# Feed-forward sums in a decoder step: three of four accumulating transfers of each pair's first half of rows are cut in two

## The chip, the cores and the metric

One core of one Trainium2 chip. The metric is the device time of one execution in microseconds (us). Engines as the profile names them: PE (TensorE, matmul), PEld (its weight loads), DVE (VectorE), ACT (ScalarE), POOL (GpSimd) and SP (SyncE). Transfers run on 16 DMA engines.

## The reference, cut to what matters

One layer of a recurrent decoder, for 1024 new tokens of a prompt and 8 single tokens (1032 tokens together), model width 1024, feed-forward width 2816, everything in float32:

```
x = x + 0.5 * swiglu(rmsnorm(x, n1), f1g, f1u, f1d)     # first feed-forward
h = rmsnorm(x);  proj = h @ w_in                        # mixer: two recurrent branches, gates
x = x + m @ w_out
x = x + 0.5 * swiglu(rmsnorm(x, n3), f2g, f2u, f2d)     # second feed-forward
y = rmsnorm(x, final_norm)

def swiglu(x, w_gate, w_up, w_down):
    return (silu(x @ w_gate) * (x @ w_up)) @ w_down
```

The change touches the two feed-forwards alone, and in them the way in which the products with w_down reach x.

## The kernel before, in words

**Layout and tiles.** Activations lie transposed: x is 8 tiles of 128 rows (of the model width) by 1032 tokens. The tokens are taken in two halves of 516 (HW), each as two banks of 258. The feed-forward width is 22 tiles of 128, taken in 11 pairs (PAIRS). Every float32 product is three matmuls with split operands (`three`, lines 149 to 156: high by high, high by low, low by high).

**A pair.** For pair i TensorE makes the gate products, then the down products of the pair before, then the up products. Each set is made with seven block products in place of eight (a 2 x 2 block scheme), whose results VectorE and ScalarE put together: ScalarE copies a bank into a tile (`snap`, line 921; `down_part`, line 929), VectorE adds another bank to it (`mix`, line 1080; `down_part`, line 1088). Pair 0 and the last pair's down products go another way, so 9 groups (i = 2 to 10) of each feed-forward have such a down stage, 18 in all. The groups 2 to 9 are a loop on TensorE, ScalarE and VectorE; GpSimd's list is written out.

**The down stage.** Its result has 8 tiles of rows. They are made in two halves, c = 0 (tiles 0 to 3, "the first half of rows") and c = 1. In each half the seven products j = 0 to 6 run, each for q = 0 and then q = 1 (which two of the four tiles), and give four parts, kind 0 to 3 (a tile of the two, a half of the tokens). A part is a tile of 128 x 2 x 516 numbers, the middle index being q. The parts of c = 0 and c = 1 share their buffers `s.part[kind]`, except that kind 2 of c = 1 lies in `snap_t[:, 1:3]`, which the up products' copies use right after (line 921, n = 1 and 2).

**Adding to x.** x itself is overlaid by other tiles while the pairs run. Ahead of them GpSimd copies x into x_sum in HBM (line 1258, eight transfers of 516 KB), and each finished part is added there by an accumulating transfer that GpSimd issues (line 1269), in the order c = 0 kinds 0, 1, 2, 3, then c = 1 kinds 0, 1, 2, 3. Each waits until both q of its part are done: kinds 0 to 2 for VectorE's sum (semaphore `mixed`), kind 3 for ScalarE's copy (`snap`). At the end SP reads x_sum back into x (lines 1316 to 1319).

**Who waits for a transfer.** Each kind has a semaphore `x_added[kind]`, 16 for each transfer landed. ScalarE's `down_part` waits on it ahead of line 929, so that a part's buffer isn't written over while it is being sent: a copy for c = 1 waits for the transfer of c = 0 of its kind (not kind 2, whose c = 1 buffer is another), a copy for c = 0 for the pair before. ScalarE's `snap` of the up products (line 921, n = 1, 2) waits for kind 2 of c = 1. TensorE then waits for these copies (`chain_wait`, `product7`): the second up product (j = 1) for the copies of kind 3, c = 1, and the fifth (j = 4) for the copy n = 1 of line 921. VectorE (line 1112, pair 1), ScalarE (line 835) and SP wait on the same semaphores once in a feed-forward.

**The other traffic.** SP loads the weights in slabs of 512 KB into two buffers (line 1280), each when the buffer is free.

Of the kernel before, what the change touches and what calls it, by code (L numbers as in the profile page):

```python
# [19 lines left out]
ALU = mybir.AluOpType  # L20
# [15 lines left out]
PAIRS = FT // 2  # L36
# [19 lines left out]
HW = T // 2  # L56
# [4 lines left out]
FIRST_PRODUCTS = 8  # L61
LAST_DOWN = 3
DOWN_PAIRS = ((3, 2), (1, 0))
ADDED = 32 * (PAIRS - 1)
PARTS = ((0, 0), (1, 1), (1, 0), (0, 1))
HIDDEN_FIRST = ((0, 0), (0, 1), (1, 0), (1, 1))
HIDDEN = ((0, 0), (1, 1), (1, 0), (0, 1))
# [203 lines left out]
def half(h):  # L271

    return slice(h * HW, (h + 1) * HW)
# [7 lines left out]
def halves(ap):  # L281

    return ap.rearrange("p (g q) -> p g q", g=2)


def both(k, pair):

    return k.pair[pair][:, :, 0:QW]


def is_one(i):

    return isinstance(i, int) and i == 1


def units(i, n):

    return FIRST_UNITS + n if is_one(i) else i * 21 + (n + FIRST_UNITS + 14 - 42)


def prods(i, n):

    return FIRST_PRODUCTS + n if is_one(i) else i * 42 + (n + FIRST_PRODUCTS + 14 - 84)


def summed(i, n):

    return n if is_one(i) else i * 12 + (n + 8 - 24)


def snaps(i, n):

    return n if is_one(i) else i * 22 + (n + 6 - 44)


def mixes(i, n):

    return n if is_one(i) else i * 18 + (n + 6 - 36)
# [14 lines left out]
def prod_number(i, up, j):  # L333
    return (0, 7 if is_one(i) else 35)[up] + j + 1
# [6 lines left out]
def mix_number(i, up, n):  # L341
    return (0, 3 if is_one(i) else 15)[up] + n + 1


def down_prod(c, j, q):
    return 7 + 14 * c + 2 * j + q + 1


def down_snap(c, n, q):

    return 3 + 8 * c + 2 * n + q + 1


def down_mix(c, n, q):

    return 3 + 6 * c + 2 * n + q + 1
# [467 lines left out]
def hidden_part(i, n):  # L824
    return (HIDDEN_FIRST if i == 0 else HIDDEN)[n]


def hidden_high(act, k, s, i, n):

    f, h = hidden_part(i, n)  # L830
    act.wait_ge(s.hidden, i * 4 + (n + 1))
    if i and n == 0:
        act.wait_ge(k.x_added[1], s.added_base + ADDED)
        act.wait_ge(k.x_added[2], s.added_base + ADDED - 16)
    act.activation(s.hid_hi[:, f, half(h)], s.gt[:, f, half(h)], ACT.Copy).then_inc(s.hidden_hi, 1)


# [7 lines left out]
def hid_f(s, j):  # L845

    return s.hb_f[:, 2 * HID_IN.get(j, j) + 1, :]
# [34 lines left out]
def ffn_scalar(act, k, s):  # L882
# [31 lines left out]
    def snap(i, up, n):  # L914
        act.wait_ge(s.prod, prods(i, prod_number(i, up, (0, 2, 3)[n])))
        if up:
            act.wait_ge(s.mixed, mixes(i, (1, 3, 2)[n]))
            if n and not is_one(i):
                act.wait_ge(k.x_added[2], i * 32 + s.added_base)
        pair = ((0, 0, 1), (2, 2, 1))[up][n]  # L920
        act.activation(halves(s.snap_t[:, n, :]), both(k, pair), ACT.Copy).then_inc(s.snap, 1)

    def down_part(i, c, n, q):

        kind = (0, 2, 1, 3)[n]
        act.wait_ge(s.prod, prods(i, down_prod(c, (0, 2, 3, 6)[n], q)))
        act.wait_ge(k.x_added[kind], i * 32 + (s.added_base - 32 + (16 * c if kind != 2 else 0)))
        pair = DOWN_PAIRS[c ^ (n == 2)][q]
        act.activation(halves(part(s, c, kind)[:, q, :]), both(k, pair), ACT.Copy).then_inc(s.snap, 1)  # L929

# [10 lines left out]
    def group_one():  # L941
        i = 1
        for j in range(2, 6):
            unit_high(act, k, s, i, 0, j)
        snap(i, 0, 0)
        unit_high(act, k, s, i, 0, 6)
        unit_high(act, k, s, i, 2, 0)
        snap(i, 0, 1)
        silu(i, 0)
        unit_high(act, k, s, i, 2, 1)  # L950
        snap(i, 0, 2)
        unit_high(act, k, s, i, 2, 2)
        unit_high(act, k, s, i, 2, 3)
        silu(i, 1)
        unit_high(act, k, s, i, 2, 4)
        silu(i, 2)
        silu(i, 3)
        unit_high(act, k, s, i, 2, 5)
        unit_high(act, k, s, i, 2, 6)
        behind_up(i, False)  # L960
# [76 lines left out]
def ffn_vector(dve, k, s):  # L1037
# [52 lines left out]
    def hidden(i, n, last):  # L1090

        f, h = HIDDEN[n]
        gt = s.gt[:, f, half(h)]
        dve.wait_ge(s.silu, i * 4 + (n + 1))
        if n < 3:
            dve.wait_ge(s.mixed, mixes(i, mix_number(i, 1, n)))
            other = s.snap_t[:, (0, 2, 1)[n], :]
        else:
            dve.wait_ge(s.prod, prods(i, prod_number(i, 1, 6)))
            other = both(k, 2)  # L1100
        if last:
            if n == 3:
                gt = halves(gt)
            dve.tensor_tensor(gt, gt, other, ALU.mult).then_inc(s.hidden, 1)
            return
        to = hid_f(s, (B11, B22, B21, B12)[n])
        if n == 3:
            gt, to = halves(gt), halves(to)
        if is_one(i) and n == 0:
            for kind in range(4):  # L1110
                dve.wait_ge(k.x_added[kind], s.added_base + 32)
        dve.scalar_tensor_tensor(to, gt, 0.5, other, ALU.mult, ALU.mult).then_inc(s.hidden, 1)

    def add(first, t, m):
# [123 lines left out]
def part(s, c, kind):  # L1238

    return s.snap_t[:, 1:3, :] if c == 1 and kind == 2 else s.part[kind][:, :, :]  # L1240


def x_block(s, c, kind):

    e, h = PARTS[kind]
    return s.x[:, 4 * c + e:4 * c + e + 3:2, half(h)]


def x_sum_block(s, c, kind):
    return s.x_sum[4 * c + kind].rearrange("p (q t) -> p q t", q=2)  # L1250


def ffn_gpsimd(pool, k, s):

    pool.wait_ge(s.down_used, NT * KT)
    for c in range(2):
        for kind in range(4):
            pool.dma_start(x_sum_block(s, c, kind), x_block(s, c, kind)).then_inc(k.x_added[kind], 16)
    for kind in range(4):
        pool.wait_ge(k.x_added[kind], s.added_base + 32)  # L1260

    def group(i):
        for c in range(2):
            for kind in range(4):
                if kind < 3:
                    pool.wait_ge(s.mixed, mixes(i, down_mix(c, kind, 1)))
                else:
                    pool.wait_ge(s.snap, snaps(i, down_snap(c, 3, 1)))
                pool.dma_start(s.x_sum[4 * c + kind], part(s, c, kind).rearrange("p q t -> p (q t)"), accum_op=ALU.add)\
                    .then_inc(k.x_added[kind], 16)  # L1270

    for i in range(2, PAIRS):
        group(i)


def ffn_sync(sp, k, s, behind_first=None, behind_second=None):

    def load(number, buf):
        src = k.w_slabs[bass.ds(number, 1)].rearrange("a p c -> p (a c)")
        sp.dma_start(k.raw[buf][:, :], src).then_inc(k.slab_loaded[buf], 16)  # L1280

    s.raw_free(sp, 0)
    load(s.first, 0)
    if behind_first:
        behind_first()
    s.raw_free(sp, 1)
    load(s.first + 1, 1)
    if behind_second:
        behind_second()
    for c in range(2, FIRST_SLABS):  # L1290
        sp.wait_ge(s.unit_lo, 2 * c - 2)
        load(s.first + c, c % 2)

    for c, done in enumerate((FIRST_UNITS - 1, FIRST_UNITS)):
        sp.wait_ge(s.unit_lo, done)
        load(s.first + FIRST_SLABS + c, c)
    for c, done in enumerate((2, 6)):
        sp.wait_ge(s.unit_lo, units(1, done))
        if c == 0:
            sp.wait_ge(s.sums, summed(1, 4))  # L1300
        load(s.first + FIRST_SLABS + 2 + c, c)

    def row(i, n, c):
        sp.wait_ge(s.unit_lo, units(i, 7 * (n - 1) + (2, 6)[c]))
        if c == 0:
            sp.wait_ge(s.sums, summed(i, 4 * n))
        load(i * 6 + (s.first - 2 + 2 * n + c), c)

    for i in range(2, PAIRS):
        for n in range(3):  # L1310
            for c in range(2):
                row(i, n, c)
    for c in range(2):
        row(PAIRS, 0, c)
    sp.wait_ge(s.prod, prods(PAIRS - 1, 35))
    for kind in s.back_order:
        sp.wait_ge(k.x_added[kind], s.added_base + ADDED)
        for c in range(2):
            sp.dma_start(x_block(s, c, kind), x_sum_block(s, c, kind)).then_inc(k.x_back[PARTS[kind][1]], 16)

# [1703 lines left out]
def build(nc, x_t, w_slabs, lru_w, vec, state_hgrn, state_lru, state_conv, consts,  # L3024
          y_out, hgrn_p, hgrn_s, lru_out, conv_p, conv_s):
    k = Names(w_slabs=w_slabs, state_hgrn=state_hgrn, hgrn_p=hgrn_p, hgrn_s=hgrn_s, lru_w_in=lru_w)
# [213 lines left out]
    with ExitStack() as ctx:  # L3240
# [3 lines left out]
        def sem(name):  # L3244
            return ctx.enter_context(nc.semaphore(name))
# [17 lines left out]
        hidden_hi, hidden_lo = sem("hidden_hi"), sem("hidden_lo")  # L3263
# [1 line left out]
        k.x_back = [sem("x_back"), k.consts_loaded]  # L3265

        def ffn(n):
            return dict(hidden_hi=hidden_hi, hidden_lo=hidden_lo, hid_base=8 * n, added_base=ADDED * n,
                        back_base=(64 * n, 32 + 64 * n), x_sum=x_sums[n])
        par = stage("par", "arg exp", steps=0)  # L3270
        n1 = stage("n1", "squared squared_vector added rstd_step " + HEAD, gain=G1, x=k.x1, x_loaded=x_loaded,
# [225 lines left out]
```

## Time and profile before

| | |
|---|---|
| Time, median of 3 runs | 2433.44 us (2432.48 to 2433.78) |
| The profiled execution | 2431.43 us, span 2429.6 us |
| PE busy | 2415.5 us (99%) |
| DVE, ACT, POOL busy | 1740.3 (72%), 1298.9 (53%), 171.9 us (7%) |
| Granted TensorE clock | 0.999 of full speed |
| q0, GpSimd's transfers | 23040 packets, 84.55 MB, 18.3% of 16 engines |
| q1, SP's transfers | 114128 packets, 192.39 MB, 24.2% |
| x_sum transfers of parts | 126 (f_part) and 18 (f_snap), 516 KB each |

The span is the profiled part of the execution; the execution's own time has some 2 us around it. Matmuls overlap (each is shown with some 0.28 us, while one starts every 0.12 us), so a stop of TensorE is seen in the starts. A row of a timeline gives start, duration, engine, line, operation, tiles, and in brackets the idle time before it and what ended it. GpSimd's rows are issues: the time that it spends on one, not the transfer.

### The profile page before, as it was taken

To read this page: it belongs to the slowest core of one execution; us is meant where nothing else is said; L and a number is where in the kernel's file an instruction comes from. 1 tells how busy PE (TensorE), PEld (TensorE's weight loads), DVE (VectorE), ACT (ScalarE), POOL (GpSimd) and SP (SyncE) were. 2 spreads that over 40 slices of the span, in tenths; PEclk is the share of its full clock that TensorE was granted. 3 is DMA by queue.
4 is the path that set the end of the run, shared out by engine and by line. 5 is a ranking of instruction groups with operands and counts; after the bars stand their busy time and mean duration, and the time that the engine had idled before them with its cause. 6 is when DMAs were issued, how large, how long until landed. Compare 5 with 4: busy or idle time off the path is not lost.

```text
span 2429.6 us, 51528 instructions
## 1 busy us (share of the span) xinstructions
PE 2415.5 (99%) x19220; PEld 2401.3 (99%) x19220; DVE 1740.3 (72%) x2921; ACT 1298.9 (53%) x2206; POOL 171.9 (7%) x204
## 2 busy tenths in 40 slices
PE   9999999999999999999999999999999999999998
PEld 8999999999999999999999999999999999999997
DVE  8767777777689888787777775442676777777777
ACT  5355555555568676676666664211434555555554
POOL 0011111111120000000000000000200111111110
PEclk9999999999999999999999999999999999999999
DMA  3355555555541343333222235332033555555556
GB/s 144 106 123 121 121 121 121 122 121 122 142 175 54 97 113 79 87 97 107 105 87 87 73 140 180 138 126 87 18 106 90 121 122 123 121 123 123 122 123 194
DMA packets 137270, 278.34 MB, mean 115 GB/s; under 512 B 67024, under 2 KB 71632, under 8 KB 136656
## 3 DMA queue, kind: packets, MB, share of 16 engines
q1 hardware_dynamic: 114128, 192.39, 24.2%
q0 software_dynamic: 23040, 84.55, 18.3%
q8 instruction: 69, 1.13, 0.2%
q14 instruction: 33, 0.27, 0.0%
HBM read 154.80 MB, written 114.77 MB: 111 GB/s over the span
## 4 chain that ended last, share of the span: by engine, by line
PE 97%; DVE 1%; ACT 1%; DMA 1%; issue 0%; SPq 0%; DVEq 0%; ACTq 0%
PE banks L154 31%; PE banks L155 31%; PE banks L156 31%; PE banks L1817 1%; PE banks L1848 1%; PE banks L1838 1%; PE banks L1852 1%; PE banks L1846 1%; DMA x_sum<-f_part 0%; DVE y L247 0%; DVE f_blk_f L502 0%; DVE f_blk_lo L526 0%; DMA raw<-w_slabs 0%; PE banks L238 0%; PE banks L240 0%; ACT f_blk_hi L518 0%
## 5 line engine op out<-in xcount | busy, mean ns | idle before, releaser
L154 PE MATMUL banks<-f_blk_hi,f_u_hi 128*128 128x258 f32 x2496 | 706.6, 283 | 1.1 <-ACT f_part L929 0.7
L155 PE MATMUL banks<-f_blk_lo,f_u_hi 128*128 128x258 f32 x2496 | 705.7, 283 | 0.0
L156 PE MATMUL banks<-f_blk_hi,f_u_lo 128*128 128x258 f32 x2496 | 704.8, 282 | 0.0
L154 PE MATMUL banks<-mix_blk_hi,mix_u_hi 128*128 128x258 f32 x1808 | 515.1, 285 | 0.7 <-DVE mix_blk_lo L526 0.4
L155 PE MATMUL banks<-mix_blk_lo,mix_u_hi 128*128 128x258 f32 x1808 | 511.0, 283 | 0.0
L156 PE MATMUL banks<-mix_blk_hi,mix_u_lo 128*128 128x258 f32 x1808 | 510.2, 282 | 0.0
L154 PEld LDWEIGHTS banks<-f_blk_hi,f_u_hi 128*128 128x128 f32 x2496 | 471.4, 189 | 2.5 <-ACT f_part L929 0.9
L156 PEld LDWEIGHTS banks<-f_blk_hi,f_u_lo 128*128 128x128 f32 x2496 | 471.2, 189 | 0.0
L155 PEld LDWEIGHTS banks<-f_blk_lo,f_u_hi 128*128 128x128 f32 x2496 | 470.9, 189 | 0.2
L154 PEld LDWEIGHTS banks<-mix_blk_hi,mix_u_hi 128*128 128x128 f32 x1808 | 342.0, 189 | 1.4 <-issue 1.1
L155 PEld LDWEIGHTS banks<-mix_blk_lo,mix_u_hi 128*128 128x128 f32 x1808 | 341.6, 189 | 0.1
L156 PEld LDWEIGHTS banks<-mix_blk_hi,mix_u_lo 128*128 128x128 f32 x1808 | 341.4, 189 | 0.0
L154 PE MATMUL banks<-f_hb,f_u_hi 128*128 128x258 f32 x1008 | 285.3, 283 | 0.0
L155 PE MATMUL banks<-f_hb,f_u_hi 128*128 128x258 f32 x1008 | 284.9, 283 | 0.0
L156 PE MATMUL banks<-f_hb,f_u_lo 128*128 128x258 f32 x1008 | 284.5, 282 | 0.0
L1088 DVE TENSOR_TENSOR f_part<-banks,f_part 128x516 f32<-128x516 f32 x180 | 125.0, 695 | 152.8 <-PE banks L156 148.6
L929 ACT ACTIVATE f_part<-banks 128x516 f32<-128x516 f32 x252 | 151.1, 602 | 103.9 <-PE banks L156 79.4
L155 PEld LDWEIGHTS banks<-f_hb,f_u_hi 128*128 128x128 f32 x1008 | 191.1, 190 | 0.0
L156 PEld LDWEIGHTS banks<-f_hb,f_u_lo 128*128 128x128 f32 x1008 | 190.5, 189 | 0.0
L154 PEld LDWEIGHTS banks<-f_hb,f_u_hi 128*128 128x128 f32 x1008 | 190.3, 189 | 0.0
L800 DVE TENSOR_TENSOR f_u_lo<-f_sum,f_u_hi 128x512 fp32r<-128x512 f32 x232 | 156.0, 687 | 42.8 <-ACT f_u_hi L794 42.5
L794 ACT ACTIVATE f_u_hi<-f_sum 128x512 fp32r<-128x512 f32 x232 | 140.8, 626 | 84.7 <-PE banks L156 47.8
(306 smaller groups left out, 4378.0 us busy)
## 6 DMA issues: line engine op xcount, KB each, us to landing
raw<-w_slabs SPq DMA_DIRECT2D x220, 512.0 KB, 3.5
x_sum<-f_part POOLq DMA_DIRECT2D x126, 516.0 KB, 7.8
x_sum<-f_snap POOLq DMA_DIRECT2D x18, 516.0 KB, 10.1
x_sum<-x POOLq DMA_DIRECT2D x16, 516.0 KB, 5.7
x<-x_sum SPq DMA_DIRECT2D x16, 516.0 KB, 8.2
sg_kept<-sgt SPq DMA_DIRECT2D x8, 1032.0 KB, 5.6
sgs<-sg_kept SPq DMA_DIRECT2D x16, 516.0 KB, 4.5
x_kept<-x SPq DMA_DIRECT2D x1, 4128.0 KB, 12.1
```

The lines of the kernel that those rows point to most:

```text
L154: pe.matmul(out, wh, xh, start=start, stop=False, skip_group_check=chained)
L155: pe.matmul(out, wh, xl, start=False, stop=False, skip_group_check=chained)
L156: return pe.matmul(out, wl, xh, start=False, stop=stop, skip_group_check=chained)
L794: act.activation(s.u_hi[j][:, :], unit_source(k, s, n, j), ACT.Copy).then_inc(s.unit_hi, 1)
L800: dve.tensor_tensor(s.u_lo[j][:, :], unit_source(k, s, n, j), s.u_hi[j][:, :].bitcast(F32), ALU.subtract)\
L929: act.activation(halves(part(s, c, kind)[:, q, :]), both(k, pair), ACT.Copy).then_inc(s.snap, 1)
L1088: dve.tensor_tensor(to, both(k, pair), to, ALU.add).then_inc(s.mixed, 1)
L1817: last = pe.matmul(k.bank[5][:, 0:P], s.ke[:, tok], s.qe[:, tok], start=True, stop=True)
L1838: pe.matmul(k.bank[6][:, at], s.kt[:, n, :], s.v[:, n, :], start=True, stop=True).then_inc(s.u_ready, 1)
L1846: pe.matmul(o[:, 0:P], s.s[n % 2][:, :], s.qe[:, n * P:(n + 1) * P], start=True, stop=False, skip_group_check=True)
L1848: last = pe.matmul(o[:, 0:P], s.v[:, n, :], s.sc[n % 2][:, :], start=n == 0, stop=True, skip_group_check=True)
L1852: last = pe.matmul(o[:, P + b:P + b + 1], s.ss[:, b, :], s.qe[:, SEQ + b:SEQ + b + 1], start=True, stop=True, skip_group_check=True)
```

## The change

Kinds 0, 1 and 3 of c = 0 are sent in two transfers of 258 KB each, one for each q, each as soon as its q is ready; kind 2 of c = 0 and all of c = 1 stay whole. A pair then has 11 accumulating transfers in place of 8. The semaphores count 48 a pair for kinds 0, 1 and 3 and 32 for kind 2 (`ADDS`), and all waits on them are put on the new counts: a copy for c = 1 waits for both halves of c = 0.

```diff
-ADDED = 32 * (PAIRS - 1)
+ADDS = (48, 48, 32, 48)
+ADDED = tuple(32 + adds * (PAIRS - 2) for adds in ADDS)
...
     if i and n == 0:
-        act.wait_ge(k.x_added[1], s.added_base + ADDED)
-        act.wait_ge(k.x_added[2], s.added_base + ADDED - 16)
+        act.wait_ge(k.x_added[1], s.added_base[1] + ADDED[1])
+        act.wait_ge(k.x_added[2], s.added_base[2] + ADDED[2] - 16)
...
             if n and not is_one(i):
-                act.wait_ge(k.x_added[2], i * 32 + s.added_base)
+                act.wait_ge(k.x_added[2], i * ADDS[2] + s.added_base[2])
...
-        act.wait_ge(k.x_added[kind], i * 32 + (s.added_base - 32 + (16 * c if kind != 2 else 0)))
+        added = s.added_base[kind] + 32 - 2 * ADDS[kind] + (32 * c if kind != 2 else 0)
+        act.wait_ge(k.x_added[kind], i * ADDS[kind] + added)
...
+    def done(i, c, kind, q):
+        if kind < 3:
+            pool.wait_ge(s.mixed, mixes(i, down_mix(c, kind, q)))
+        else:
+            pool.wait_ge(s.snap, snaps(i, down_snap(c, 3, q)))
+
     def group(i):
         for c in range(2):
             for kind in range(4):
-                if kind < 3:
-                    pool.wait_ge(s.mixed, mixes(i, down_mix(c, kind, 1)))
+                to = s.x_sum[4 * c + kind]
+                if c == 0 and kind != 2:
+                    for q in range(2):
+                        done(i, c, kind, q)
+                        pool.dma_start(to[:, q * HW:(q + 1) * HW], part(s, c, kind)[:, q, :], accum_op=ALU.add)\
+                            .then_inc(k.x_added[kind], 16)
                 else:
-                    pool.wait_ge(s.snap, snaps(i, down_snap(c, 3, 1)))
-                pool.dma_start(s.x_sum[4 * c + kind], part(s, c, kind).rearrange("p q t -> p (q t)"), accum_op=ALU.add)\
-                    .then_inc(k.x_added[kind], 16)
+                    done(i, c, kind, 1)
+                    pool.dma_start(to, part(s, c, kind).rearrange("p q t -> p (q t)"), accum_op=ALU.add)\
+                        .then_inc(k.x_added[kind], 16)
```

The remaining lines of the diff put the same new counts into the waits of VectorE (line 1112), SP (line 1316) and the start of GpSimd's list.

## Rows read from the trace of the kernel before

**Rows 1.** The page: busy time by engine; the chain that ended last, by engine
```profile
PE 2415.5 (99%) x19220; PEld 2401.3 (99%) x19220; DVE 1740.3 (72%) x2921; ACT 1298.9 (53%) x2206; POOL 171.9 (7%) x204
...
PE 97%; DVE 1%; ACT 1%; DMA 1%; issue 0%; SPq 0%; DVEq 0%; ACTq 0%
```

**Rows 2.** Waits of TensorE, whole span: us in total, times, longest
```profile
PE banks L154 <- ACT f_part L929: 0.7, 1, 0.7
```

**Rows 3.** Timeline of PE around 1889 us
```profile
1888.94 0.28 PE L155 MATMUL banks<-f_blk_lo,f_u_hi 128*128 128x258 f32 x1
1889.06 0.28 PE L156 MATMUL banks<-f_blk_hi,f_u_lo 128*128 128x258 f32 x1
1890.04 0.39 PE L154 MATMUL banks<-f_blk_hi,f_u_hi 128*128 128x258 f32 x1 [0.70 <-ACT f_part L929]
```

**Rows 4.** Timeline of ACT, the same pair
```profile
1888.89 1.09 ACT L929 ACTIVATE f_part<-banks 128x516 f32<-128x516 f32 x2 [3.18 <-DMA x_sum<-f_part]
```

**Rows 5.** Timeline of POOL: the copies of x; one pair; the late pair
```profile
89.07 2.29 POOL L1258 DMA_DIRECT2D x_sum<-x  x3 [87.14 <-DVE x L1120]
93.89 0.70 POOL L1258 DMA_DIRECT2D x_sum<-x  x1 [2.53 <-issue]
...
217.70 0.84 POOL L1269 DMA_DIRECT2D x_sum<-f_part  x1 [2.98 <-DVE f_part L1088]
...
220.50 0.85 POOL L1269 DMA_DIRECT2D x_sum<-f_part  x1 [0.48 <-ACT f_part L929]
223.47 0.85 POOL L1269 DMA_DIRECT2D x_sum<-f_part  x1 [2.12 <-DVE f_part L1088]
...
229.25 0.88 POOL L1269 DMA_DIRECT2D x_sum<-f_snap  x1 [0.60 <-DVE f_snap L1088]
232.57 0.85 POOL L1269 DMA_DIRECT2D x_sum<-f_part  x1 [2.45 <-issue]
...
1877.44 0.84 POOL L1269 DMA_DIRECT2D x_sum<-f_part  x1 [0.46 <-ACT f_part L929]
```

**Rows 6.** Us to landing, issues at 89.07, 217.70, 220.50, 223.47, 229.25, 1877.44
```profile
x_sum<-x POOLq DMA_DIRECT2D x1, 516.0 KB, 4.5
...
x_sum<-f_part POOLq DMA_DIRECT2D x1, 516.0 KB, 5.4
...
x_sum<-f_part POOLq DMA_DIRECT2D x1, 516.0 KB, 7.7
...
x_sum<-f_part POOLq DMA_DIRECT2D x1, 516.0 KB, 8.7
...
x_sum<-f_snap POOLq DMA_DIRECT2D x1, 516.0 KB, 9.5
...
x_sum<-f_part POOLq DMA_DIRECT2D x1, 516.0 KB, 11.4
```

**Rows 7.** Timeline of DVE, the pair around 217 us
```profile
215.93 2.85 DVE L1088 TENSOR_TENSOR f_part<-banks,f_part 128x516 f32<-128x516 f32 x4 [0.62 <-PE banks L156]
```

**Rows 8.** Queues' packets, MB, share: windows 221 to 223, 91 to 93, 668 to 670
```profile
q0 software_dynamic: 115, 0.41, 107.8%
...
q0 software_dynamic: 174, 0.65, 96.6%
...
q1 hardware_dynamic: 412, 0.81, 104.9%
```

**Rows 9.** All waits of line 921; its copies and PE's next matmuls, two pairs
```profile
ACT f_snap L921 <- DMA x_sum<-f_snap: 64.5, 18, 4.1
...
238.87 0.60 ACT L921 ACTIVATE f_snap<-banks 128x516 f32<-128x516 f32 x1 [2.92 <-DMA x_sum<-f_snap]
...
240.88 0.28 PE L154 MATMUL banks<-f_blk_hi,f_u_hi 128*128 128x258 f32 x1
...
2079.45 0.60 ACT L921 ACTIVATE f_snap<-banks 128x516 f32<-128x516 f32 x1 [4.08 <-DMA x_sum<-f_snap]
...
2080.29 0.29 PE L154 MATMUL banks<-f_blk_hi,f_u_hi 128*128 128x258 f32 x1
```

More of the change, by code:

```diff
@@ L1110, in hidden @@
             for kind in range(4):
-                dve.wait_ge(k.x_added[kind], s.added_base + 32)
+                dve.wait_ge(k.x_added[kind], s.added_base[kind] + 32)
         dve.scalar_tensor_tensor(to, gt, 0.5, other, ALU.mult, ALU.mult).then_inc(s.hidden, 1)
@@ L1259, in ffn_gpsimd @@
     for kind in range(4):
-        pool.wait_ge(k.x_added[kind], s.added_base + 32)
+        pool.wait_ge(k.x_added[kind], s.added_base[kind] + 32)
+    def done(i, c, kind, q):
[3 more added lines that the diff above has]
+            pool.wait_ge(s.snap, snaps(i, down_snap(c, 3, q)))
     def group(i):
@@ L1316, in ffn_sync @@
     for kind in s.back_order:
-        sp.wait_ge(k.x_added[kind], s.added_base + ADDED)
+        sp.wait_ge(k.x_added[kind], s.added_base[kind] + ADDED[kind])
         for c in range(2):
@@ L3267, in ffn @@
         def ffn(n):
-            return dict(hidden_hi=hidden_hi, hidden_lo=hidden_lo, hid_base=8 * n, added_base=ADDED * n,
+            return dict(hidden_hi=hidden_hi, hidden_lo=hidden_lo, hid_base=8 * n, added_base=tuple(added * n for added in ADDED),
                         back_base=(64 * n, 32 + 64 * n), x_sum=x_sums[n])
```

## The prediction

> **What bounds the kernel now.** I read the page's totals and chain first, then the waits of TensorE, then the timelines around the transfers that change, then their landings.
>
> The reader is to see that TensorE is never done: busy 2415.5 of 2429.6 us and 97% of the chain of waits, with VectorE, ScalarE and DMA at 1% each [rows 1]. So the change can only pay by removing idle time of TensorE, and cost by making some. In the list of TensorE's waits just one entry has to do with the changed transfers: one wait of 0.7 us, for line 929, the copy of a finished part out of a bank [rows 2]. It lies in the second feed-forward, in the first of its pairs that has a down product. Up to there one matmul starts every 0.12 us (1888.94, 1889.06); the next starts at 1890.04 instead of 1889.18, so 0.86 us are lost [rows 3]. ScalarE explains it: at 1888.89 it begins the two copies of part 3 for the second half of rows, after 3.18 us of waiting for an x_sum transfer, and 1.09 us later (1889.98) they are done [rows 4]. That transfer is part 3 of the first half of rows, issued at 1877.44 [rows 5] and landed 11.4 us later, at 1888.84 [rows 6].
>
> I write K0 to K3 for the four transfers of the first half of rows and K0' to K3' for those of the second. The change splits K0, K1 and K3.
>
> **The change, part by part.** I take the first feed-forward's pair around 217 us as the pattern; 17 of the 18 pairs show no loss on TensorE. K0 goes 2.98 + 0.85 us ahead of K1 [rows 5] and is nearly out when K1's data come: its split moves nothing behind it.
>
> *The earlier first halves.* VectorE's four part instructions from 215.93 take 2.85 us, 0.71 each [rows 7]; the second ends at 217.36 and K1 is issued at 217.70 [rows 5]. The first half of K1 is ready 0.71 us sooner and can go at 216.99. The issue keeps GpSimd 0.84 us, so the second half goes at about 217.84, 0.14 later than K1 now. K1 lands 5.4 us after its issue, at 223.1 [rows 5, 6]. K3 (220.50 + 7.7) lands at 228.2, so K2 and K3 follow K1 in 5.1 us, 2.55 each [rows 5, 6]: from K1 on the transfers stand in line and the DMA engines set the pace.
>
> *Cost of a half on the engines.* The trace has no accumulating row piece of 2,064 bytes. From three windows of 2 us: accumulating pieces of 4,128 bytes take 1.078 x 2 us x 16 engines / 0.41 MB = 84 engine-us per MB, 0.35 us each; plain pieces of 4,128 bytes 0.966 x 2 x 16 / 0.65 = 48 per MB; plain pieces of 2,064 bytes (x read back) 1.049 x 2 x 16 / 0.81 = 41 per MB [rows 8]. Plain pieces are thus not dearer by the byte when they are halved. Below, a halved accumulating piece costs 0.35 x 41/48 / 2 = 0.15 us (each split K gains 8 x 2 x 0.025 = 0.4 us); above, as much as a whole one, 0.35 (each split K costs 8 x 0.35 = 2.8 us more). I take half, 0.175, being nearest to the plain rows: a split costs nothing in line.
>
> *When K1 and K3 then land.* A half alone should land 5.4 - 1.3 = 4.1 us after its issue: the first at 221.1, the second 1.35 us behind at 222.4 against 223.1, 0.65 us earlier. K2 and K3 follow, 0.65 us earlier too.
>
> *What GpSimd's queue adds.* GpSimd seems to have room for three transfers: of the eight plain copies the first three go back to back from 89.07 and the fourth at 93.89, 0.32 us after the first landed (89.07 + 4.5); K3' is ready early but goes at 232.57, 0.40 us after K0' landed (223.47 + 8.7) [rows 5, 6]. If a half takes a place like a whole, the first half of K3 waits for that of K1 (221.1 + 0.3 = 221.4), the second for the second of K1 (222.7), and K0' for K2 (225.75 - 0.65 + 0.3 = 225.4, now 223.47). A transfer alone spends 5.4 - 2.7 = 2.7 us outside its service, so their data are ready at the latest at 224.1, 225.4 and 228.1, while the line before them is worked on until about 225.1, 226.4 and 227.5. Only K0' can find an empty line, for 0.6 us at most, which gives back what was won. Behind the held issues on GpSimd stand only its own later transfers. So K2' comes between 0.65 us earlier and no later than now.
>
> *Who waits for that.* K2' is the transfer with the least room: every pair ScalarE's copy on line 921 waits for it, 64.5 us in 18 times, up to 4.1 [rows 9]. After the 2.92 us wait the copy ends at 238.87 + 0.60 = 239.47 and the matmul that needs its bank starts at 240.88, 1.41 us spare; after the 4.08 us wait it is 2080.05 against 2080.29, 0.24 us spare [rows 9]. Spare time is thus 4.32 less the wait, 0.74 us in the mean (64.5 / 18 = 3.58). An earlier K2' gives nothing: TensorE doesn't stall there. It is what hides the 54 added issues (18 pairs x 3); once it is used up, each us later costs up to 18 us.
>
> *The rest.* GpSimd gets 54 x 0.85 = 46 us more issue time, three in the pair; it has 2 to 3 us idle between issues [rows 5], and nothing else sits on it in these stretches. ScalarE, VectorE and SP wait as often as before, on other numbers; ScalarE's copies for the second half now need both halves landed, which is when they needed the whole. I put these at nothing.
>
> *The sum.* The late pair: its K1 to K3 go 0.65 us earlier, K3 at 1888.2, copies done at 1889.3, matmul at 1889.4, so 0.2 of the 0.86 us stay: 0.66 us won, once. Against the profiled execution: 2431.43 (span 2429.6 and 1.8 around it) - 0.66 = 2430.8. The median of the runs, 2433.44, lies 2.0 above the profiled one; on that scale 2432.8.
>
> The Trainium skill has a rule against splitting: "DMA: Bandwidth & Descriptors", section on the anatomy of one SWDGE DMA, gives a transfer issued by GpSimd a fixed 2.0 us plus its bytes at 436 GB/s, 3.2 us for 516 KB. The trace agrees for a transfer alone (5.4 us, more even) and not for one in line, 2.55 us behind the one before [rows 5, 6].
>
> **Rivals.**
> 1. *The loss stays.* The one late K3 is late because the line in that pair is slow as a whole (11.4 us against 7.7 [rows 6]), and held issues eat the head start. For: it happens in 1 of 18 pairs, which the size of a transfer doesn't explain. Against: K1 is ahead of it in any case. Time 2433.4, or 1 us either way.
> 2. *Slower: three places are too few.* K0' held for K2, or K3's halves for K1's, leaves the engines empty more than I computed, in all pairs. It decides from an empty 0.65 + 0.74 = 1.4 us a pair on, where K2' comes 0.74 us late and spare time is gone in the mean; single pairs pay from 0.9. At 2 us it costs about 18 x (2 - 1.4) = 11 us: 2444; at 1.4 some 3 us: 2436. For: the holds in rows 5. Against: 2.7 us of work stands in line when a place comes free.
> 3. *Slower: a halved piece costs like a whole one.* Two splits stand ahead of K2' in the line (K1, K3): 2 x 2.8 - 0.65 = 4.9 us later, 18 x (4.9 - 0.74) = 75 us: 2508. Against: plain pieces go by the byte [rows 8].
> 4. *A fixed time for each added transfer in line.* If two more starts were paid ahead of K2' as a transfer alone pays (2.7 us outside its service each), 5.4 - 0.65 - 0.74 = 4.0 us a pair, 72 us: 2505. Against: K2 and K3 pay no such time now. By the 2.0 us that the Trainium skill gives in "DMA: Bandwidth & Descriptors" it would be 18 x (2 x 2.0 - 0.65 - 0.74) = 47 us: 2480.
>
> **How the numbers follow.** Forecast 0.62; rival 1 0.20; rival 2 0.11; rivals 3 and 4 together 0.06; something faster that I don't see 0.01, as no more than 0.86 us of TensorE's idle time hangs on these transfers. A measurement tells 0.2%, 4.9 us, from no change. The forecast, rival 1 and half of rival 2 are inside it: 0.88; slower 0.11; faster 0.01. The range goes from 2430.6 (all 0.86 us won, and two us for the spread between medians) to 2438.0 (rival 2 up to its middle).
>
> **What would show it.** GpSimd should show 198 accumulating issues, 108 halves (258 KB) and 90 wholes, for the 144 now, of some 0.85 us each. In the pair around 217 us K1's second half should land near 222.4, K3's near 227.5, and K2' not after 238.75 (229.25 + 9.5 [rows 5, 6]); the wait of line 921 on x_sum should be at or under 64.5 us in sum. The price of a 2,064-byte accumulating piece, read as above from a window of the line: 84 engine-us per MB or less if I am right, near 170 if rival 3 is. K0' should be seen to go about 0.3 us after K2 lands if places are counted by transfer, at 223.47 if by bytes. TensorE's one wait on line 929 should shrink to some 0.2 us or go, with no new entry on line 921 or 929. The prediction is wrong if TensorE waits on line 921 or 929 in several pairs, or if the time leaves the range; if the time fits and the 0.7 us wait is still there, its mechanism is wrong and rival 1 right.

## The result, and the profile after

Changed, the kernel takes 2482.98 us (median of 5 runs, 2479.79 to 2487.96) against 2432.48 (5 runs, 2431.72 to 2433.78): a ratio of 1.0207, 95% interval 1.0196 to 1.0219. Some 50 us are lost. 2432.8 was forecast, so the prediction was wrong.

Numbers are written as in the prediction (K0 to K3, K0' to K3'; a and b are the two halves of a split transfer). Lines after line 63 have moved by 1 to 12: the copy of a part (929) is now 931, the copy for the up products (921) is 922, the accumulating issues (1269) are 1277 for halves and 1281 for wholes.

The page after, busy time, GpSimd's queue (packets, MB, share of 16 engines), the chain that ended last, the issues (KB each, us to landing); the first and third answer to [rows 1]:

```profile
PE 2430.3 (98%) x19220; PEld 2408.8 (97%) x19220; DVE 1741.0 (70%) x2921; ACT 1293.4 (52%) x2206; POOL 218.3 (9%) x258
...
q0 software_dynamic: 30816, 84.56, 20.4%
...
PE 87%; DMA 7%; issue 2%; DVE 2%; ACT 1%; POOL 0%; SPq 0%; ACTq 0%; DVEq 0%
...
x_sum<-f_part POOLq DMA_DIRECT2D x72, 516.0 KB, 7.7
x_sum<-f_part POOLq DMA_DIRECT2D x108, 258.0 KB, 4.7
```

GpSimd issues 108 halves and 90 wholes (72 and the 18 from `f_snap`), as it should. But DMA now has 7% of the chain that TensorE alone held. TensorE's waits after, which answer to [rows 2], and ScalarE's behind them (us in total, times, longest):

```profile
PE banks L155 <- ACT f_part L931: 24.7, 18, 2.1
PE banks L155 <- ACT f_snap L922: 8.7, 11, 1.5
```
```profile
ACT f_snap L922 <- DMA x_sum<-f_snap: 80.5, 17, 5.9
ACT f_part L931 <- DMA x_sum<-f_part: 66.2, 17, 4.6
```

One late copy of 0.7 us has become one in each of the 18 pairs, and 11 more behind it. In the pattern pair (its down stage now begins at 213.22 us, before at 209.14) the views of [rows 3, 4] show the stop; first PE, then ACT:

```profile
236.21 0.28 PE L157 MATMUL banks<-f_blk_hi,f_u_lo 128*128 128x258 f32 x1
238.06 0.39 PE L155 MATMUL banks<-f_blk_hi,f_u_hi 128*128 128x258 f32 x1 [1.56 <-ACT f_part L931]
238.28 0.29 PE L156 MATMUL banks<-f_blk_lo,f_u_hi 128*128 128x258 f32 x1
```
```profile
236.91 1.09 ACT L931 ACTIVATE f_part<-banks 128x516 f32<-128x516 f32 x2 [4.09 <-DMA x_sum<-f_part]
```

ScalarE's two copies of part 3 for the second half of rows start 4.09 us late, at 236.91, because K3b has landed only at 236.82; TensorE's second up product needs them and starts at 238.06. The starts are 1.85 us apart where 0.12 is usual, so the stop is 1.73 us, 0.17 more than the wait that the view counts, and the next start comes 0.10 late too.

The loss adds up so: waits 24.7 + 8.7 = 33.4 us; 29 stops with 0.27 us each beside the wait, if all are as this one, 7.8; and the clock. After four of the longer stops (1.8 to 2.1 us) the granted clock shows its lower level for 3.4 us, as here from 302.1 us (windows: us, busy time and instructions of PE, PEld, DVE, ACT, POOL, granted clock, DMA share, GB/s):

```profile
300.00:302.00 2.00, 0.38 (x3) 0.38 (x4) 0.00 (x0) 1.52 (x4) 1.34 (x2) 1.00 0.92 275
302.00:305.50 3.50, 3.50 (x19) 3.50 (x18) 1.39 (x2) 1.10 (x3) 1.24 (x2) 0.51 1.09 187
305.50:308.00 2.50, 2.50 (x23) 2.50 (x22) 1.56 (x3) 0.63 (x1) 0.00 (x0) 1.00 1.02 168
```

TensorE had stopped in the first window (0.38 us busy of 2), and the 0.51 of the second is 1.2 GHz in place of 2.4. In that stretch matmuls start every 0.215 us in place of 0.12 (302.29, 302.51, 302.72 in the timeline), so it loses 1.5 us, and four of them lose 6.0. Together 47.2, of the 48.4 by which the span has grown.

GpSimd's issues of the pair, which answer to [rows 5] (the second half of K0, then K1 to K3'), and the us to landing of those at 218.04, 223.13 and 227.55, to [rows 6]:

```profile
218.04 0.85 POOL L1277 DMA_DIRECT2D x_sum<-f_part  x1 [0.45 <-DVE f_part L1090]
221.07 0.84 POOL L1277 DMA_DIRECT2D x_sum<-f_part  x1 [2.17 <-DVE f_part L1090]
223.13 0.88 POOL L1277 DMA_DIRECT2D x_sum<-f_part  x1 [1.22 <-DVE f_part L1090]
223.67 1.22 POOL L1281 DMA_DIRECT2D x_sum<-f_part  x1
227.55 1.72 POOL L1277 DMA_DIRECT2D x_sum<-f_part  x2 [2.66 <-issue]
232.00 0.87 POOL L1281 DMA_DIRECT2D x_sum<-f_part  x1 [2.72 <-DVE f_part L1090]
237.09 0.85 POOL L1281 DMA_DIRECT2D x_sum<-f_part  x1 [4.22 <-issue]
237.63 1.19 POOL L1281 DMA_DIRECT2D x_sum<-f_snap  x1
```
```profile
x_sum<-f_part POOLq DMA_DIRECT2D x1, 258.0 KB, 4.8
...
x_sum<-f_part POOLq DMA_DIRECT2D x1, 258.0 KB, 4.1
...
x_sum<-f_part POOLq DMA_DIRECT2D x1, 258.0 KB, 7.4
```

The reader is to see who waits for whom. K1b goes at 223.13, 0.26 us after K0b landed (218.04 + 4.8, by the landing event 222.87); K2 goes straight behind it; K3a and K3b go together at 227.55, 0.33 us after K1b landed (223.13 + 4.1, by the event 227.22); K1' and K2' go together at 237.09, 0.27 us after K3b landed. The prediction had each issue wait for the transfer three before it. Here issues come in twos, each two behind both halves of a split part.

From the trace's landing events, medians over the 18 pairs, us after the start of the down stage (in the pattern pair before the change, K3 has until 21.9 us and K2' until some 31.0 before TensorE's second and fifth up product must stop: the product starts at 23.11 and 31.74, less ScalarE's two copies, 1.09, or its one, 0.60, and about 0.1):

```
kernel                         time us   K3 issued  landed   K2' issued  landed   PE waits for copies of K3 / K2', us
before                         2432.5    11.32      19.20    20.10       30.39     0.7 /  0
K0 split                       2432.50   11.21      19.12    20.12       30.54     0   /  0.6
K0, K1 split, own semaphores   2437.37   12.41      21.25    21.58       31.04     1.5 /  1.4
K3 split, own semaphore        2441.48   14.28 (b)  22.07    22.37       31.31     3.3 /  0.7
all three, own semaphores      2448.49   14.61 (b)  21.90    22.16       31.38     2.7 /  6.5
all three, 64-row halves       2449.30   11.76 (b)  22.79    23.07       31.72    14.1 /  0.3
K1 split                       2457.17   14.26      22.77    23.04       31.70    18.1 /  0
K3 split                       2467.17   14.38 (b)  22.01    22.81       32.53     2.2 / 22.5
changed                        2482.98   15.18 (b)  23.44    24.24       33.29    24.7 /  8.7
```

(b) is the second half. Where K3 lands near or behind its limit TensorE waits for the copies of K3, and where K2' does for those of K2'.

### The profile page after: what moved, and what is told of

Read it like the earlier page. It is cut to its first block, busy times and chain, and to the rows that moved or that the text cites. A ratio compares the mean times of both kernels' runs of the same rounds, so it can differ in the third digit from the quotient of the medians.

```text
span 2478.0 us, 51582 instructions
## 1 busy us (share of the span) xinstructions
PE 2430.3 (98%) x19220; PEld 2408.8 (97%) x19220; DVE 1741.0 (70%) x2921; ACT 1293.4 (52%) x2206; POOL 218.3 (9%) x258
## 3 DMA queue, kind: packets, MB, share of 16 engines
q0 software_dynamic: 30816, 84.56, 20.4%
## 4 chain that ended last, share of the span: by engine, by line
PE 87%; DMA 7%; issue 2%; DVE 2%; ACT 1%; POOL 0%; SPq 0%; ACTq 0%; DVEq 0%
PE banks L155 28%; PE banks L156 28%; PE banks L157 28%; DMA x_sum<-f_snap 4%; DMA x_sum<-f_part 2%; PE banks L1829 1%; PE banks L1860 1%; PE banks L1850 1%; PE banks L1864 1%; PE banks L1858 0%; DVE y L248 0%; POOL x_sum L1281 0%; DVE f_snap L1090 0%; DVE f_blk_f L503 0%; DMA raw<-w_slabs 0%
## 5 line engine op out<-in xcount | busy, mean ns | idle before, releaser
L155 PE MATMUL banks<-f_blk_hi,f_u_hi 128*128 128x258 f32 x2496 | 713.8, 286 | 33.8 <-ACT f_part L931 24.7
```

Source lines behind the costliest of these rows:

```text
L155: pe.matmul(out, wh, xh, start=start, stop=False, skip_group_check=chained)
```

## The experiments

Two theories run through the experiments. **P, places**: GpSimd's queue holds so many pieces (a piece is one row's 4,128 or 2,064 bytes), a further issue is held until a landing frees a place, and transfers that count on one semaphore give their places back together. **F, a fixed price**: each added transfer costs the line 1 to 2.5 us, wherever it stands. Later came **C**: the weight load that SP issues 15.2 us after the stage's start takes engines just when a late K3 is under way. The expectations of the first four runs (own semaphores, 64-row halves, 256 pieces, K1 alone) were written before these letters and carry their own: A1 there is P with places counted by transfer, A2 the same without the semaphores, B a dearer small piece, and C there is F.

**1. Semaphores of their own for the first halves.** To make room, three seldom used semaphores are merged into others.

```diff
-                            .then_inc(k.x_added[kind], 16)
+                            .then_inc((k.x_first, k.x_added)[q][kind], 16)
```

> The changed kernel, but the first halves of K0, K1 and K3 count on semaphores of their own (three seldom used semaphores of the mixer are merged to make room). Theory A1 (GpSimd's queue has three places, and a place whose transfer shares its semaphore with a later one comes free only when both have landed): K1's second half is issued some 8.7 us after the down stage begins and not at 9.9, K3's halves near 12.3 and 13.6 and not at 14.3 and 14.9; the time comes back to 2435 us, within 5. Theory A2 (three places, semaphores don't matter): issues and time as in the changed kernel, 2483 within 6. Theory B (an accumulating piece of 2,064 bytes costs more than half of one of 4,128) and theory C (a fixed time for each transfer in line): 2483 within 6, whatever the issues do.

Measured: 2448.49 us, ratio 1.0066 (1.0048 to 1.0084). GpSimd's issues of K1a and K1b, K3a, K3b and K0' in this kernel's pattern pair (it starts at 212.07):

```profile
220.00 1.75 POOL L1277 DMA_DIRECT2D x_sum<-f_part  x2 [2.36 <-DVE f_part L1090]
...
224.41 0.85 POOL L1277 DMA_DIRECT2D x_sum<-f_part  x1 [1.42 <-ACT f_part L931]
226.72 0.85 POOL L1277 DMA_DIRECT2D x_sum<-f_part  x1 [1.45 <-ACT f_snap L931]
229.26 0.87 POOL L1281 DMA_DIRECT2D x_sum<-f_part  x1 [1.70 <-issue]
```

K1b no longer stands behind K0b: it goes right after K1a. K3a goes 0.32 us after K1a landed (224.09), K3b 0.26 after K1b, K0' 0.31 after K2: all three transfers back, and singly. Nothing but the semaphores differs from the changed kernel, and two thirds of the loss are gone. So the issues go as A1 says (medians: K1b at 8.5 us, K3a at 12.35; K3b at 14.6, not 13.6) and A2, B and C, which ask for 2483, are out as the whole cause; but A1's 2435 within 5 is missed as well, and 16 us of loss are left. The control, the kernel before with the merged semaphores alone:

> The kernel before with the three seldom used semaphores merged into others, as the runs with semaphores of their own need it, and nothing else: no theory expects a difference, 2431.5 to 2433.5 us. Should it be slower, the losses of those runs are smaller by as much.

Measured: 2431.73 us, ratio 1.0000 (0.9990 to 1.0009). So the merging costs nothing.

**2. What a place is.** Two kernels change the number of pieces. One cuts the split parts by rows: 64 rows with pieces of 4,128 bytes, both halves sent when the whole part is ready.

```diff
-                    for q in range(2):
-                        done(i, c, kind, q)
-                        pool.dma_start(to[:, q * HW:(q + 1) * HW], part(s, c, kind)[:, q, :], accum_op=ALU.add)\
+                    done(i, c, kind, 1)
+                    for rows in (slice(0, P // 2), slice(P // 2, P)):
+                        pool.dma_start(to[rows], part(s, c, kind)[rows].rearrange("p q t -> p (q t)"), accum_op=ALU.add)\
```

> The changed kernel, but the two transfers of K0, K1 and K3 are the upper and the lower 64 rows, both issued when the whole part is ready: as many transfers and waits, pieces of 4,128 bytes. Theories A1 and A2 (places): holds as in the changed kernel, and no head start, so 2470 to 2500 us. Theory B (pieces of 2,064 bytes): back to 2433 within 4. Theory C (fixed time for each transfer): 2483 within 8.

The other leaves eight transfers and gives K0, K1 and K3 256 pieces of 2,064 bytes each (x_sum is laid out anew, so the two pieces of a row aren't neighbours).

```diff
+    if c == 0 and kind != 2:
+        return s.x_sum[4 * c + kind].rearrange("p t -> (p t)").rearrange("(q p t) -> p q t", q=2, p=P)
```

> The kernel before, with its eight transfers a pair, but x_sum of K0, K1 and K3 laid out so that each goes in 256 pieces of 2,064 bytes in one transfer (read and written back in the same order). Theories A1, A2 and C (number of transfers): 2433 us within 4. Theory B (small pieces): slower by more than 20 us, 2455 to 2490.

Measured: 2449.30 us, 1.0066 (1.0048 to 1.0084), and 2500.94 us, 1.0275 (1.0257 to 1.0293). The issues of the second (K0; K1 and K2; K3; K0'; K1'):

```profile
218.48 1.20 POOL L1271 DMA_DIRECT2D x_sum<-f_part  x1 [41.10 <-DVE f_part L1088]
224.53 2.15 POOL L1271 DMA_DIRECT2D x_sum<-f_part  x2 [4.85 <-issue]
230.88 1.19 POOL L1271 DMA_DIRECT2D x_sum<-f_part  x1 [4.20 <-issue]
233.49 0.92 POOL L1271 DMA_DIRECT2D x_sum<-f_part  x1 [1.42 <-DVE f_snap L1088]
238.69 0.85 POOL L1271 DMA_DIRECT2D x_sum<-f_part  x1 [4.28 <-issue]
```

With no transfer added this is the slowest of the kernels so far: K1 waits for K0 alone (landed 224.26), K3 for K1 (230.57). A transfer of 256 pieces fills two places, so two of them don't fit at once. The halves of 64 rows go the other way: K0a to K2, five transfers, go without a hold, and so does K3a. It goes some 0.3 us after ScalarE's copy of its part is done, in four of the 18 pairs only 0.05 to 0.19 us after K0b's landing, while a held issue starts at least 0.25 us after the landing that frees it. If K0a and K0b give their places back together, as in 1., they still had them then, and 64 x 4 + 128 + 64 = 448 pieces had found room. 512 never did, in any pair of any kernel: not 128 more on three transfers of 128, and not two transfers of 256. One rule fits all issues: room for 448 pieces or somewhat more, under 512, freed when all transfers on a semaphore have landed. Counted in pieces, theory P stands; how the queue does it isn't seen.

None of the theories had either time: A1 and A2 asked for 2470 to 2500 and 2433, C for 2483 and 2433, B for 2433 and at most 2490. The 64-row kernel also shows that holds aren't all. Nothing is held there ahead of K3, and yet K1b lands at 16.0 us (K1 before: 14.05) and K3b at 22.8 (19.2).

**3. Which split costs.** Each part alone, with the change's own semaphores.

```diff
-ADDS = (48, 48, 32, 48)
+SPLIT = (1,)                        # (0,) and (3,) in the two others
+ADDS = tuple(48 if kind in SPLIT else 32 for kind in range(4))
```

> The changed kernel with K1 alone in two halves (nine transfers a pair). Theory A1: K2 is held until K0 has landed (10.4 us after the down stage begins), K3 until both halves of K1 have (13.8), no hold behind that; the line hardly runs empty: 2433 to 2442 us. Theories B and C: a third to a half of the loss, 2450 to 2458.

> Only part 0 in two halves, both on the semaphore of their part, as in the change. Theory P: both halves have landed (7.8 and 9.8 us) before any later transfer needs their place, so no issue is held for them, part 3 lands at 19 to 20 us and the time is that of before: 2432 to 2434 us. If every split had its price (the loss of 50 us shared by three): 2440 to 2449 us.

> Of the first half's transfers only that of part 3 goes in two, both halves on the semaphore of their part, as in the change. Theory P (places): the line has room for three transfers of 128 pieces, each further issue waits for a landing, and two transfers of one semaphore give their places back together. Then the first half of part 3 goes at 10.3 to 11.4 us after the down stage's start, the second at about 14.3 (0.3 us after part 1's landing at 14.0), it lands by 21 us, before the 21.9 us that TensorE's second up product can stand, and the later transfers are held about 2.5 us longer: 2434 to 2442 us. Theory F (each added transfer has a fixed price in the line, 1 to 2.5 us by the spacing of 1.8 to 2.5 us in which halves landed): part 3 of the first half lands at 20.1 to 21.6 us, part 2 of the second at 30.6 to 32.1 against 31.0: 2433 to 2453 us. Both allow a small loss here; the issue and landing times tell them apart.

Measured: K1 alone 2457.17 us, 1.0114 (1.0088 to 1.0139), with the issues as A1 has them (medians: K2 at 10.4 us, K3 at 14.3) but a time that lies in the range of B and C; K0 alone 2432.50, 1.0001 (0.9991 to 1.0010); K3 alone 2467.17, 1.0143 (1.0126 to 1.0160). K0's split is free, as P says: both halves have landed before a later transfer wants their place. K1's and K3's cost 25 and 35 us, and each in its own spot of the pair. With K1 split, K3 itself is held (issued at 14.26 instead of 11.32) and TensorE waits 18.1 us for part 3's copies. With K3 split, K3b lands at 22.01, just at the limit, but the hold falls on K1' and K2'. The two lines of GpSimd that show it (first K0', K1', K2' with the shared semaphore, then the same three with K3a on its own):

```profile
228.84 0.88 POOL L1282 DMA_DIRECT2D x_sum<-f_part  x1 [1.76 <-issue]
234.22 0.85 POOL L1282 DMA_DIRECT2D x_sum<-f_part  x1 [4.50 <-issue]
234.76 1.19 POOL L1282 DMA_DIRECT2D x_sum<-f_snap  x1
```
```profile
227.15 0.88 POOL L1282 DMA_DIRECT2D x_sum<-f_part  x1 [1.87 <-issue]
229.10 0.85 POOL L1282 DMA_DIRECT2D x_sum<-f_part  x1 [1.08 <-DVE f_part L1091]
232.84 0.85 POOL L1282 DMA_DIRECT2D x_sum<-f_snap  x1 [2.88 <-issue]
```

K1' stands 4.50 us for K3b in the first, although K3a landed 4 us earlier (230.18); in the second it goes as soon as its data are there. P's expectation for K3 alone, 2434 to 2442, had that hold but priced it as 2.5 us on transfers with room for it; they had none. F's 2433 to 2453 is missed too. The second kernel:

> As the run that splits part 3 alone, but its first half has a semaphore of its own (three seldom used semaphores are merged into others to make room). Theory P: every hold is for the transfer three before, no pair is freed together, so part 1 of the second half is no longer held for both halves of part 3: 2432.5 to 2436 us, below the run on a shared semaphore. Theory F: the price in the line does not depend on semaphores: the same time as that run, within 0.2%.

Measured: 2441.48 us, 1.0039 (1.0025 to 1.0054). F, which asks for the time of the shared semaphore, is out by 26 us; P's 2432.5 to 2436 is too low by 5.5. And K0 and K1 split, on their own semaphores:

> Parts 0 and 1 of the first half in two, part 3 whole, first halves on semaphores of their own. Theory P: part 3 is held for the landing of the first half of part 1 (about 12.0 us after the down stage's start), goes at 12.3 instead of 11.4 us and lands at about 20.6, within the 21.9 us that there are: 2432.5 to 2437 us, so nearly the whole 16 us that the run with all three splits on own semaphores still lost come from part 3's split. Theory F: two added transfers put part 3's landing 2 to 5 us behind 19.1, at 21.1 to 24.1: up to 2.2 us a pair, 2433 to 2472 us, and of those 16 us two thirds stay, about 2443.

Measured: 2437.37 us, 1.0020 (1.0010 to 1.0029), 0.4 above P's range, and inside F's wide one, 6 under the 2443 that F names; K3 is issued at 12.41 us as P expected and lands at 21.25, 0.6 later than P had it. Own semaphores leave 5 us of loss with two splits, 9 with K3's, 16 with all three.

**4. The price of a half in the line.** All halves of K0, K1 and K3 are kept back until part 3 is ready, so that they stand one behind the other.

```diff
                     for q in range(2):
+                        done(i, c, 3, 1)
                         done(i, c, kind, q)
```

> As the run with all three splits on own semaphores, but no half of the first half of rows is sent before part 3 is ready, so that the halves stand in the line one behind the other. Its time is not the point (TensorE must stop about 5 us in every pair: 2510 to 2560 us). Read is the spacing of landings of the second half of part 0, both halves of part 1 and those of part 3 while two or more transfers are ahead of them. If a half costs by its bytes (0.18 us a piece, 8 pieces on each of 16 engines) it is 1.3 to 1.6 us; if each transfer has a fixed price, near that of a whole one, 2.0 to 2.5 us; if the slow first pieces belong to a transfer that starts soon after its issue, 1.3 to 1.6 us for those that stood 3 us or longer and about 1 us more for the first.

Measured: 2588.72 us, 29 above the range that the expectation gave for the time. Medians over the pairs: K0b lands 2.67 us behind K0a, then K1a 1.29 behind K0b and K1b 1.30 behind K1a; wholes in a full line land 2.5 apart in every kernel (K3' behind K2'). So a half that stands in line costs half, and F is wrong there. The halves of K3 don't show it: K3a lands 2.71 us behind K2 and K3b 1.74 behind K3a, but there the weight load is under way as well (its first packet comes at 23.8 us after the stage's start, K3a lands at 27.8); without it, in 5., they land 1.3 and 1.5 us behind. Yet the line of the changed kernel as a whole does more work than before: 20.4% of 16 engines over 2478.0 us in its page against 18.3% of 2429.6, 505.5 - 444.6 = 61 us, or 1.1 us for each of the 54 added transfers. K2 lands 4.2 us behind K1b in the kernel that keeps the halves back and 4.0 in the changed one. A stretch of the changed kernel shows what that is; the queue's packets, MB and share from 226 to 228 us, while K2 starts behind K1b's last pieces:

```profile
q0 software_dynamic: 88, 0.21, 120.9%
```

1.209 x 2 us x 16 / 0.21 MB is 184 engine-us per MB, over twice the 84 of [rows 8]: the engines are at work, but single pieces take up to 2.35 us. They are K2's first pieces, which start while K1b's last are still under way. By the share of the page the three kernels without pair holds pay about 0.7 to 0.8 us for each added transfer, some 0.1 either way by the page's rounding (K0 alone 18.8% of 2430.4; K3 alone on its own semaphore 18.8% of 2439.6; K0 and K1 on theirs 19.4% of 2437.0). Part of it is the piece: a median of 0.18 us for 2,064 bytes against 0.331 for 4,128 in the trace makes a split part 0.23 us dearer (128 x (2 x 0.18 - 0.331) / 16). The rest is slow pieces. Why a start is slow isn't settled.

**5. The weight load.** SP's load, which goes 15.2 us after the stage's start, waits for K3 in addition; in the changed kernel, and in the one before.

```diff
         if c == 0:
             sp.wait_ge(s.sums, summed(i, 4 * n))
+        if n == 0 and c == 0:
+            sp.wait_ge(k.x_added[3], i * 48 + (s.added_base[3] - 80))
```

> The change, and the weight load that SyncE issues 15.2 us after the down stage's start (512 KB, on another queue, over the same 16 engines) waits in addition for the landing of the first half's part 3. Theory C (the weight load takes the engines just when the late part 3 is under way, and is a part of the price): the two halves of part 3, which landed 3.3 and 1.9 us behind the transfer before them, land 1.3 to 2.0 us behind it, the second at 20.8 to 22.0 us instead of 23.6; TensorE's waits for the copies of part 3 fall from 24.7 us to under 8 us, and the time to 2440 to 2465 us. Theory P alone (only the holds for places count): part 3 still lands at 23 us or later and the time stays at 2475 us or above. If the load, now about 6 us later, makes weights late, TensorE waits for the weights' splitting instead, and the run after this one shows the same.

> The kernel before with that same wait of the weight load for the first half's part 3 (19.1 us after the down stage's start, so 4 us later than now). Theory C: part 0 of the second half, which lands 4.0 us behind part 3, lands about 2.5 us behind it; nothing waits for that, so 2431 to 2434 us. If a load 4 us later makes weights late: 2440 us or more.

Measured: 2501.07 us, 1.0275 (1.0250 to 1.0300), and 2436.91 us, 1.0017 (1.0008 to 1.0027). Theory C has K3's landings right and the time wrong; the second kernel falls between its two expectations. The two queues while K3a and K3b are served, in the changed kernel from 231.7 to 236.8 us, and with the load held from 231.1 to 234.2:

```profile
q0 software_dynamic: 308, 0.74, 78.3%
q1 hardware_dynamic: 138, 0.50, 27.1%
```
```profile
q0 software_dynamic: 267, 0.57, 123.5%
```

With the load out of the way the halves of K3 land 1.3 and 1.5 us behind what precedes them (medians; 3.1 and 1.9 in the changed kernel), K3b at 21.01 in place of 23.44, and TensorE's wait for part 3's copies is gone. But the load then meets K0' and K1', K2' lands at 33.56, and TensorE stands there instead:

```profile
PE banks L155 <- ACT f_snap L922: 44.4, 18, 3.9
```

So the collision is 2.4 us of K3's delay, and nothing is gained by holding the load back: even before the change, a load 4 us later costs 5 us.

## Why the prediction was wrong

**What failed first: "Only K0' can find an empty line, for 0.6 us at most".** It rested on places that come free one by one, three transfers back. The rows on which it stood ([rows 5, 6]) are all of transfers whose predecessor on the same semaphore had long landed, so they couldn't show that two transfers on one semaphore free their places together. In the changed kernel K1b is held for K0b, K3a and K3b for K1b, K1' and K2' for K3b: K3b goes at 15.2 us (median) where K3 went at 11.3, and K2' at 24.2 for 20.1. Own semaphores, with all else kept, take back 34 of the 50 us. This is rival 2's mechanism, though without the semaphores; its holds were named ("K3's halves for K1's"), and its 2436 to 2444 were far too cheap.

**"A split costs nothing in line" was mis-sized.** The piece itself was right: halves that stand in line land 1.29 us apart, 0.16 us a piece on each engine, by the 0.175 taken. What was left out are starts. The prediction had K1b land 1.35 us behind K1a and 0.65 earlier than K1 before; it lands 2.3 us behind K1a and 0.3 later, with its hold (14.31 against 14.05) and without it, on own semaphores (14.35). So nothing was won at the front of the line. Each added transfer takes 0.7 to 0.8 us more engine time without pair holds and 1.1 in the changed kernel. Three of 1.1 are 3.4 us a pair against the 0.74 us of spare time that the prediction had itself worked out.

**"K2' is the transfer with the least room" looked at the wrong end.** K3 of the first half had 2.7 us (19.2 against 21.9) and K2' 0.6 to 0.7. That is why K2' was followed and K3 not; but K3 lands 4.2 us later, by the holds, the starts and the weight load together, more than its room, and the 24.7 us on line 931 are the larger part of TensorE's 33.4 us of waits. The prediction had named such waits as what would show it wrong.

**Rivals 3 and 4.** Rival 3 is out: a half in line costs 1.29 us and its piece 0.18 in the median, 87 engine-us per MB where rival 3 asked for near 170 (and the prediction for 84 or less). Rival 4 asked 2.7 us in line for each added transfer, and a half in a full line shows no such time. Rival 4's aside, worked out from the fixed 2.0 us that the Trainium skill gives a transfer issued by GpSimd ("DMA: Bandwidth & Descriptors", anatomy of one SWDGE DMA), came to 2480, near the 2483 measured. By the runs that is chance: a half in a full line costs 1.3 us in all, an added transfer 0.7 to 1.1 us of the line, and two thirds of the loss go away with semaphores on which that figure doesn't depend.

**What came out as said.** 198 issues of some 0.85 us; K0' held for K2 (in the pattern pair it goes 0.33 us after K2's landing), so a half of 128 pieces takes a place like a whole.

**The weight load wasn't in the sum.** The Trainium skill ("DMA: Bandwidth & Descriptors", section "Queues, rings and completion order") says that each engine takes turns between the queues that have work. The trace agrees as far as both queues are served in the same stretch: with 0.50 MB of weights between them the halves of K3 take 5.1 us of line, without them 3.1. Before the change K3 had landed at 19.2 us, and the load's first packet came at 19.0 (median), so the load fell on K0', which TensorE didn't wait for. In the changed kernel that packet comes at 16.5, K3b lands at 23.4, and K3 itself runs into the load.

What stays open: why first pieces behind a short line take up to 2.35 us, and how much of the last 16 us (own semaphores, all three split) is due to that and how much to the holds that are left there.

## What to carry over

Before cutting a GpSimd transfer in two, count what may stand in its queue: a half with as many rows takes a whole place, and two halves on one semaphore give both places back only when the second has landed. If a split must be, give each half a semaphore of its own, and cut where nothing later wants the place (K0 here, which is free). Ask of every transfer behind the cut how much later it may land, not only of the one with the least room, and what other traffic it will meet there.

## What the runs showed of the hardware

- GpSimd's queue took 384 pieces of accumulating transfers, and 448 in the 64-row kernel if its pairs give their places back together; it never took 512. A held issue went 0.25 to 0.45 us after the landing that freed it.
- Places of two transfers on one semaphore came free together, at the later landing: 34 us of 2483 hung on that.
- A transfer of 256 pieces that is issued alone keeps GpSimd 1.20 us instead of 0.85 and lands 5.8 us after its issue (128 pieces: 5.4); two of them never stood in the queue at once.
- After stops of some 2 us TensorE's granted clock stood at 0.5 for 3.41 us, four times in the changed kernel. Before the change it stood there only at the end of the span.
